# A fused two-block transformer kernel: state-space tables and sums moved to GpSimd, and the first norm's squares added by pairs

## What is computed

```python
def rms_norm(x, gain):
    y = x * rsqrt(mean(x * x, axis=-1) + EPS)
    return y * gain

def s5_mixer(h, w_in, lam_re, lam_im, log_step, b_re, b_im, c_re, c_im, d_skip, w_glu):
    u = (h @ w_in).reshape(bsz, seq, 64, 16)            # 64 groups of 16 channels
    step = exp(log_step)[:, None]
    a = exp(lr * step) * (cos(li * step) + i sin(li * step))   # 64 states in a group
    f = (a - 1) / (lr + i li)
    b = f * (b_re + i b_im)
    x_t = a * x_(t-1) + b @ u_t                           # along the sequence
    y = real(c @ x_t) + d_skip * u
    z = gelu(y)
    val, gate = split(z @ w_glu)
    return val * sigmoid(gate)

x = x + s5_mixer(rms_norm(x, mix_norm[0]), ...)
```

## Time and profile before

| | |
|---|---|
| median of 3 runs | 1765.92 us (1765.71 to 1766.07) |
| the profiled execution, its own time | 1765.68 us |
| its span | 1763.9 us |
| PE busy | 1734.0 us (98%) |
| DVE busy | 1244.0 us (71%) |
| ACT busy | 924.6 us (52%) |
| POOL busy | 486.6 us (28%) |
| granted TensorE clock | 0.998 of 2.4 GHz |

### The profile page before, as it was taken

How to read it: one execution, slowest core, us unless ns; L and a number is a source line. 1 busy time by engine, 2 the same in 40 slices (tenths; PEclk the granted TensorE clock), 3 DMA queues, 4 the chain that set the end, 5 groups by cost and what they waited for, 6 DMA issues and landing times.

```text
span 1763.9 us, 27676 instructions
## 1 busy us (share of the span) xinstructions
PE 1734.0 (98%) x10382; PEld 1420.9 (81%) x10382; DVE 1244.0 (71%) x1895; ACT 924.6 (52%) x1692; POOL 486.6 (28%) x383
## 2 busy tenths in 40 slices
PE   9999999999999999999999999999999999999997
PEld 6778899999887787789999988688667768866775
DVE  8964488887345888768888835565777586577757
ACT  6634466565224677556566522333667543366753
POOL 0870166775001000026776500132001113200110
PEclk9999999999999999999999999999999999999999
DMA  6332323223333211022323333233111123311111
GB/s 214 94 97 84 95 72 117 100 98 119 105 94 106 75 43 37 13 96 85 108 97 119 105 98 99 82 106 98 60 48 56 57 79 107 98 60 49 59 55 55
DMA packets 56465, 151.75 MB, mean 86 GB/s; under 512 B 16768, under 2 KB 18720, under 8 KB 56336
## 3 DMA queue, kind: packets, MB, share of 16 engines
q1 hardware_dynamic: 52816, 147.45, 25.7%
q0 software_dynamic: 3520, 2.57, 0.6%
HBM read 142.84 MB, written 4.19 MB: 83 GB/s over the span
## 4 chain that ended last, share of the span: by engine, by line
PE 87%; DVE 6%; POOL 3%; ACT 2%; issue 1%; DMA 0%; SPq 0%; DVEq 0%; POOLq 0%; ACTq 0%
PE bank L2587 10%; PE bank L2588 10%; PE bank L2589 10%; PE bank L2800 8%; PE bank L2801 8%; PE bank L2802 8%; PE bank L3218 3%; PE bank L3220 3%; PE bank L3219 3%; PE bank L2883 2%; PE bank L3171 2%; PE bank L3200 2%; PE bank L3202 2%; PE bank L3201 2%; PE bank L2915 1%
## 5 line engine op out<-in xcount | busy, mean ns | idle before, releaser
L1619 DVE TENSOR_TENSOR wl<-raw,wh 128x1024 fp32r<-128x1024 f32 (+2 forms) x183 | 230.2, 1258 | 240.9 <-ACT wh L864 236.7
L864 ACT ACTIVATE wh<-raw 128x1024 fp32r<-128x1024 f32 (+2 forms) x183 | 188.6, 1031 | 354.7 <-PE bank L2589 287.3
L2587 PE MATMUL bank<-hidH,wh 128*128 128x512 f32 x352 | 137.4, 390 | 0.0
L2588 PE MATMUL bank<-hidL,wh 128*128 128x512 f32 x352 | 137.0, 389 | 0.0
L2589 PE MATMUL bank<-hidH,wl 128*128 128x512 f32 x352 | 136.9, 389 | 0.0
L2800 PE MATMUL bank<-xH,wh 128*128 128x256 f32 x480 | 135.8, 283 | 0.0
L2801 PE MATMUL bank<-xL,wh 128*128 128x256 f32 x480 | 135.8, 283 | 0.0
L2802 PE MATMUL bank<-xH,wl 128*128 128x256 f32 x480 | 135.8, 283 | 0.0
L775 POOL TENSOR_TENSOR raw<-raw,wsum 128x512 f32<-128x512 f32 x40 | 86.5, 2163 | 115.6 <-DVE wl L1948 115.6
L3218 PE MATMUL bank<-xH,wh 128*128 128x512 f32 x256 | 111.3, 435 | 0.0
L3220 PE MATMUL bank<-xH,wl 128*128 128x512 f32 x256 | 100.8, 394 | 0.0
(11 more groups left out here) (525 smaller groups left out, 5112.9 us busy)
## 6 DMA issues: line engine op xcount, KB each, us to landing
raw<-w_gu_dram SPq DMA_DIRECT2D x88, 512.0 KB, 3.6
raw<-w_p_dram SPq DMA_DIRECT2D x64, 512.0 KB, 3.3
raw<-w_dn_dram SPq DMA_DIRECT2D x32, 448.0 KB, 3.4
raw<-w_glu_dram SPq DMA_DIRECT2D x16, 512.0 KB, 3.5
raw<-w_dn_dram SPq DMA_DIRECT2D x16, 512.0 KB, 3.6
raw<-w_out_dram SPq DMA_DIRECT2D x16, 512.0 KB, 3.2
raw<-w_in_dram SPq DMA_DIRECT2D x8, 512.0 KB, 7.7
raw<-w_o_dram SPq DMA_DIRECT2D x8, 512.0 KB, 3.2
```

The lines of the kernel that those rows point to most:

```text
L864: nc.scalar.activation(wh[:, (st.base + u) % 2, 0:kts * P], raw[:, (st.base + u) % 4, 0:kts * P], ACT.Copy).then_inc(w_high, 1)
L1619: nc.vector.tensor_tensor(wl[:, s, 0:kts * P], raw[:, (st.base + u) % 4, 0:kts * P], wh[:, s, 0:kts * P].bitcast(F32), ALU.subtract).then_ ...
L2587: nc.tensor.matmul(bank, wh[:, s, w], hi[:, k, :], start=first and kt == 0, stop=False)
L2588: nc.tensor.matmul(bank, wh[:, s, w], lo[:, k, :], start=False, stop=False)
```

## The change

Five things are done together.

- POOL adds the squares by pairs in place, and PE sums four tiles with the matrix of ones, not eight.
- The turn angles (32 activations on ACT, rounding and wrapping on DVE) become three operations of 2048 elements on POOL (`make_turns`).
- `input_sums` and `output_sums` go from DVE to POOL. The negated copy of Cz goes: ACT scales by -1 when it copies.
- g(1) goes from DVE to POOL, ahead of v(0). So that the count of `g_ready` keeps its order, POOL waits within v(0) until g(0) is there and then counts g(1).
- DVE makes the low part of block 3 before `gained`, and signals `powers_ready` right behind it. ACT takes the sines earlier, beside blocks 4 and 5.

```diff
@@ gpsimd @@
-            def make_v(q):
+            def make_v(q, between=None):
...
+                if between:
+                    between()
...
+            def make_turns():
+                each = vecs[:, VEC["chunk"]:VEC["chunk"] + NCH].unsqueeze(1).to_broadcast([P, NPAIR, NCH])
+                turn = v("turn").unsqueeze(2).to_broadcast([P, NPAIR, NCH])
+                pool.wait_ge(sem("vecs_loaded"), 16)
+                pool.wait_ge(sem("lrs_ready"), 2)
+                step(nc.gpsimd.tensor_tensor(Ei[:, :, :], each, turn, ALU.mult))
+                pool.sem_inc(sem("phases_ready"), 1)
+                step(nc.gpsimd.tensor_scalar(Er[:, :, :], Ei[:, :, :], ROUND, ROUND, ALU.add, ALU.subtract))
+                nc.gpsimd.tensor_tensor(Ei[:, :, :], Ei[:, :, :], Er[:, :, :], ALU.subtract).then_inc(sem("phases_ready"), 1)
+
+            def input_sums():
+                pool.wait_ge(sem("bc_loaded"), 32)
+                step(nc.gpsimd.tensor_tensor(Bz[:, 2, :, :], Bz[:, 0, :, :], Bz[:, 1, :, :], ALU.add))
+                step(nc.gpsimd.tensor_tensor(Bz[:, 3, :, :], Bz[:, 1, :, :], Bz[:, 0, :, :], ALU.subtract))
+                pool.sem_inc(sem("pool_tables"), 1)
+
+            def output_sums():
+                step(nc.gpsimd.tensor_tensor(Cz[:, 3, :, :], Cz[:, 0, :, :], Cz[:, 1, :, :], ALU.add))
+                step(nc.gpsimd.tensor_tensor(Cz[:, 4, :, :], Cz[:, 0, :, :], Cz[:, 1, :, :], ALU.subtract))
...
+            for j in range(4):
+                pool.wait_ge(sq_ready, 2 * j + 2)
+                step(nc.gpsimd.tensor_tensor(x_square(2 * j), x_square(2 * j), x_square(2 * j + 1), ALU.add))
+                pool.sem_inc(sem("pool_tables"), 1)
+            make_turns()
+            input_sums()
+            output_sums()
             pool.wait_ge(sem("powers_ready"), 1)
+            make_g(1)
+
+            def second_inputs():
+                pool.wait_ge(sem("g_ready"), 1)
+                pool.sem_inc(sem("g_ready"), 1)
+
             pool.wait_ge(sem("sq_used"), KD)
             pool.wait_ge(sd_ready, 1)
             pool.wait_ge(sem("phases_ready"), 3)
-            make_v(0)
+            make_v(0, between=second_inputs)
@@ scalar @@
-                    for ri, c in enumerate((0, 2)):
-                        ins = nc.scalar.activation(C2[halves(h), q % 2, ri, :, h, :], Cz[halves(h), c, q * QP:(q + 1) * QP, :], ACT.Copy)
+                    for ri, sign in enumerate((1.0, -1.0)):
+                        ins = nc.scalar.activation(C2[halves(h), q % 2, ri, :, h, :], Cz[halves(h), ri, q * QP:(q + 1) * QP, :], ACT.Copy, scale=sign)
...
-            for pair in range(NPAIR):
-                ins = nc.scalar.activation(Ei[:, pair, :], each, ACT.Identity, scale=v_turn(pair))
...
+            act.wait_ge(sem("pool_tables"), 1)
+            act.wait_ge(sem("bc_loaded"), 32)
+            lag_weights(0)
+            nc.scalar.preload_act_table(ACT.Sin)
             next_block(2)
-            act.wait_ge(sem("pool_tables"), 1)
-            lag_weights(0)
+            act.wait_ge(sem("phases_ready"), 3)
+            step(nc.scalar.activation(Er[:, :, :], Ei[:, :, :], ACT.Abs))
+            nc.scalar.activation(Er[:, :, :], Er[:, :, :], ACT.Sin, scale=-TURN, bias=tiny[:, 3:4]).then_inc(sem("phases_ready"), 1)
             next_block(3)
+            nc.scalar.activation(Ei[:, :, :], Ei[:, :, :], ACT.Sin, scale=TURN).then_inc(sem("phases_ready"), 1)
+            nc.scalar.preload_act_table(ACT.Gelu_apprx_tanh)
+            lag_weights(1)
             next_block(4)
@@ vector @@
             powers(4)
+            next_block(1)
             gained()
-            next_block(1)
-            input_sums()
-            output_sums()
+            dve.sem_inc(sem("powers_ready"), 1)
             dve.wait_ge(sd_ready, 1)
             take_input(0)
             take_input(1)
             next_block(2)
+            dve.wait_ge(sem("bc_loaded"), 32)
             make_g(0, (0,))
             take_input(2)
             next_block(3)
             make_g(0, (1,))
-            wrap_turns()
             take_input(3)
             next_block(4)
             take_input(4)
-            make_g(1, (0,), between=lambda: take_input(5))
-            make_g(1, (1,))
+            take_input(5)
@@ tensor @@
-                    for k in range(KD):
-                        pe.wait_ge(sq_ready, k + 1)
-                        nc.tensor.matmul(banks[7][:, :], const("ones"), x_square(k), start=k == 0, stop=k == KD - 1)\
-                          .then_inc(sem("sq_used"), 1)
+                    for j in range(4):
+                        pe.wait_ge(sem("pool_tables"), j + 2)
+                        nc.tensor.matmul(banks[7][:, :], const("ones"), x_square(2 * j), start=j == 0, stop=j == 3)\
+                          .then_inc(sem("sq_used"), 2)
```

More of the change, by code:

```diff
@@ L694, in make_g @@
                 step(nc.gpsimd.tensor_tensor(t, ps, br, ALU.mult))
-                pool.wait_ge(sem("lag_made"), 2 * q - 3)
-                pool.wait_ge(sem("wt_ready"), 4 * q - 4)
+                if q >= 2:
+                    pool.wait_ge(sem("lag_made"), 2 * q - 3)
+                    pool.wait_ge(sem("wt_ready"), 4 * q - 4)
                 step(nc.gpsimd.tensor_tensor(to[:, 0], pi, b_sum, ALU.mult))
@@ L699, in make_g @@
                 step(nc.gpsimd.tensor_tensor(to[:, 1], pr, b_gap, ALU.mult))
-                nc.gpsimd.tensor_tensor(to[:, 1], to[:, 1], t, ALU.add).then_inc(sem("g_ready"), 1)
+                if q == 1:
+                    step(nc.gpsimd.tensor_tensor(to[:, 1], to[:, 1], t, ALU.add))
+                else:
+                    nc.gpsimd.tensor_tensor(to[:, 1], to[:, 1], t, ALU.add).then_inc(sem("g_ready"), 1)
+            def make_turns():
[15 more added lines that the diff above has]
+                step(nc.gpsimd.tensor_tensor(Cz[:, 4, :, :], Cz[:, 0, :, :], Cz[:, 1, :, :], ALU.subtract))
             def v(name):
@@ L967, in _ @@
             next_block(1)
-            act.wait_ge(sem("lrs_ready"), 2)
-            each = vecs[:, VEC["chunk"]:VEC["chunk"] + NCH]
-            for pair in range(NPAIR):
-                ins = nc.scalar.activation(Ei[:, pair, :], each, ACT.Identity, scale=v_turn(pair))
-            ins.then_inc(sem("phases_ready"), 1)
             nc.scalar.preload_act_table_set("natural_log_exp_and_others")
@@ L979, in _ @@
               .then_inc(sem("act_made"), 1)
+            act.wait_ge(sem("pool_tables"), 1)
+            act.wait_ge(sem("bc_loaded"), 32)
+            lag_weights(0)
+            nc.scalar.preload_act_table(ACT.Sin)
             next_block(2)
-            act.wait_ge(sem("pool_tables"), 1)
-            lag_weights(0)
+            act.wait_ge(sem("phases_ready"), 3)
+            step(nc.scalar.activation(Er[:, :, :], Ei[:, :, :], ACT.Abs))
+            nc.scalar.activation(Er[:, :, :], Er[:, :, :], ACT.Sin, scale=-TURN, bias=tiny[:, 3:4]).then_inc(sem("phases_ready"), 1)
             next_block(3)
+            nc.scalar.activation(Ei[:, :, :], Ei[:, :, :], ACT.Sin, scale=TURN).then_inc(sem("phases_ready"), 1)
+            nc.scalar.preload_act_table(ACT.Gelu_apprx_tanh)
+            lag_weights(1)
             next_block(4)
             copy_w(0, (0, 1))
-            lag_weights(1)
-            nc.scalar.preload_act_table(ACT.Sin)
-            act.wait_ge(sem("phases_ready"), 3)
-            step(nc.scalar.activation(Er[:, :, :], Ei[:, :, :], ACT.Abs))
             act.wait_ge(w_split, st.base + 6 + 5)
@@ L992, in _ @@
             copy_w(0, (2, 3))
-            nc.scalar.activation(Er[:, :, :], Er[:, :, :], ACT.Sin, scale=-TURN, bias=tiny[:, 3:4]).then_inc(sem("phases_ready"), 1)
             clear_lags(first_MS)
@@ L997, in _ @@
             next_block(5)
-            nc.scalar.activation(Ei[:, :, :], Ei[:, :, :], ACT.Sin, scale=TURN).then_inc(sem("phases_ready"), 1)
-            nc.scalar.preload_act_table(ACT.Gelu_apprx_tanh)
             def turned_high(q, ts=(0, 1)):
@@ L1694, in chunk_turn @@
                 nc.vector.tensor_scalar(o, o, CH / TWO_PI, None, ALU.mult).then_inc(sem("lrs_ready"), 1)
-            def wrap_turns():
-                dve.wait_ge(sem("phases_ready"), 2)
-                step(nc.vector.tensor_scalar(Er[:, :, :], Ei[:, :, :], ROUND, ROUND, ALU.add, ALU.subtract))
-                nc.vector.tensor_tensor(Ei[:, :, :], Ei[:, :, :], Er[:, :, :], ALU.subtract).then_inc(sem("phases_ready"), 1)
             def denominator():
@@ L1743, in gained, with make_g @@
                     tt(table[:, 2, :, :], table[:, 0, :, :], table[:, 1, :, :], ALU.add)
-            def input_sums():
-                dve.wait_ge(sem("bc_loaded"), 32)
-                tt(Bz[:, 2, :, :], Bz[:, 0, :, :], Bz[:, 1, :, :], ALU.add)
-                tt(Bz[:, 3, :, :], Bz[:, 1, :, :], Bz[:, 0, :, :], ALU.subtract)
-            def output_sums():
-                step(nc.vector.tensor_scalar(Cz[:, 2, :, :], Cz[:, 1, :, :], -1.0, None, ALU.mult))
```

(11 more changed lines are left out.)

## The result

| | before | after |
|---|---|---|
| median of five runs each | 1765.92 us | 1784.07 us (1783.16 to 1784.82) |
| ratio | | 1.0103, 95% interval 1.0091 to 1.0114 |
| span of the profiled execution | 1763.9 us | 1781.4 us |

The forecast was 1786.0 us with a range of 1772 to 1794. The page of the changed kernel: its first line, the busy time of each engine, and PE's granted clock in 40 slices.

The account below looks back on a forecast made before the run. PE, busy 98% of the 1763.9 us span, was taken as the bound. g(0)'s transposes 24.0 us late less 4.8 of waits made 19.2 on 1765.68, 1784.9; with 1 for the clock, 1786 us, range 1772 to 1794.

Parts of the forecast that it names:

- The mechanism: DVE operations reading two SBUF tiles wait for POOL's whole current operation, small ones included; PE stands still 24 to 43 us.
- Rivals A: DVE's small operations beside POOL are not held; PE saves 3.2 us of sums, v(2) comes 3.5 us earlier: 1762.4; 12%.
- B: DVE's chain keeps its turn and POOL out; block 2 4 us late, POOL's list 10 us later: 8 us, 1774; 12%.
- Its ending: From g(0) on the lateness stays with PE, less waits; transposes at 70 instead of 45.95, 24.0 us later.
- The pair sums: Before block 2: POOL ends the fourth at about 20.3, PE asks at 20.7; the 3.2 us saved are worth nothing.
- The rounding: In POOL's early list: one input, 2048 elements, taken as 3.0 us between bounds of 1.9 and 4.4.
- DVE gets one for each of POOL's: Beside POOL's eleven operations: 15 of DVE's 33 small ones done at 37.8 us, low part of block 2 ends at 43.3.
- the low part of block 4: On DVE before g(0): held once by POOL's g(1), started at 50, ending near 57.5.
- What comes back: Behind g(0): PE's waits whose cause is now early go, 4.8 us off the lateness.
- The four waits of the earlier trace: PE's waits for g(3), v(2), take_input and g(1), up to 130 us: 1.5 + 1.4 + 1.2 + 0.7 = 4.8 us.
- The clock: PE slower after three standstills; a restart costs nothing to 2.3 us, 1 us taken since the last standstill is short.

Follow-up runs that it names:

- pool_reads: Kernel before plus eight multiplications of 128x1024 on POOL in a scratch tile behind the chunk turn, nothing of the change: 1778.36 us, ratio 1.0070.
- pool_clears: Kernel before plus nineteen POOL memsets of a scratch tile, which write SBUF and read nothing: 1766.28 us, ratio 1.0002.
- after_no_pairs: Changed kernel with the pair sums taken out again, so PE sums eight squares: 1780.01 us, ratio 1.0081.
- am_two_inputs: Changed kernel with one small DVE operation (am = ar - 1) written with two SBUF inputs and the same value: 1781.44 us, ratio 1.0089.
- round_in_halves: Changed kernel with POOL's rounding of 2048 elements written as two of 1024: 1779.91 us, ratio 1.0078.

## Why the prediction was right, step by step

**The mechanism** is shown: the small operations are held by POOL's. It is seen in 11 rows of the changed kernel, without the change's own work in `pool_reads`, and, but for one operation, not where POOL only writes (`pool_clears`). Rivals A (small ones not held) and B (a chain of DVE keeps POOL out) are wrong: POOL never waited for the chain. Its ending was right too: the lateness of DVE's list goes on to PE.

**The pair sums** were in time and PE's 3.2 us worth nothing, as said; alone they cost 4.2 us.

**The rounding was the term that was mis-sized**: 3.0 us taken, 1.9 to 4.4 as bounds, 7.10 measured. Memset and copy were the nearest rows, but have no arithmetic; with two steps POOL takes 3.5 ns for each of the 2048 elements. POOL's list therefore ended at 41.8, not 37.8. The other operations were well priced (turn product 3.66 against 4.1, subtraction 4.54 against 4.7, sums 1.25 to 1.32).

**"DVE gets one for each of POOL's"** was wrong the other way: 21 small operations were done at the end of POOL's list, not 15. Both errors together give 44.8 + 1.2 = 46.0 for the low part of block 2 (43.3 predicted), 52.5 for the powers (49.9), and 70.6 for g(0) (69.7). In between, the low part of block 4 was predicted to be held by 2.2 us and was held by 0.2 (56.53, 1.41 us), which took back most of the lateness; its end, 57.9, is near the 57.5 predicted.

**What comes back** was too small: 4.8 predicted, and 24.7 - 17.5 = 7.2 measured (the transposes' delay less the span's growth). The four waits of the earlier trace rows went, and with them others that the prediction had not counted, of 0.7 us at lag_turned, 0.5 at a second take_input and 0.4 in two more: 6.4 in all. The last 0.8 us lie at the same places: matmul by matmul, PE's lateness falls only there, from 24.7 to 17.6 us at 111 us of the kernel before, and in most places by up to 0.2 us more than the wait (0.80 at the wait of 0.67 for g(1)).

**The clock** fell, and cost nothing in this execution. The windows of the changed kernel (stretch, length, busy time of each engine, granted clock, DMA):

```profile
24.00:28.00 4.00, 0.32 (x1) 0.00 (x0) 3.93 (x3) 1.32 (x2) 3.78 (x2) 1.00 0.00 0
28.00:46.00 18.00, 0.00 (x0) 0.00 (x0) 17.28 (x23) 0.00 (x0) 13.39 (x6) 0.51 0.00 0
46.00:52.00 6.00, 5.83 (x14) 4.62 (x15) 5.59 (x15) 0.00 (x0) 0.00 (x0) 0.50 0.57 173
52.00:56.00 4.00, 4.00 (x19) 3.26 (x18) 1.82 (x4) 3.38 (x7) 3.25 (x2) 0.97 0.37 136
```

PE stood still from 24.3, the clock was 1.00 up to 28 and 0.51 from there to 46, the level of 1.2 GHz; and block 2 ran at 0.50 for 6 us before it was 1.00 again. But PE waited 2.14 us for DVE at 67.75 and 0.65 at 70.69, so these slower 6 us are covered. Behind the standstill of 2.14 us the clock stayed at 1.00, so the 1 us for it was not due here. That is partly luck, as `after_no_pairs` shows at the same place (two rows of PE):

```profile
63.38 0.47 PE L2595 MATMUL bank<-xH,wh 128*128 128x512 f32 x1 [2.40 <-DVE wl L1650]
...
66.47 1.71 PE L2636 MATMUL bank<-cons,G 128*128 128x128 f32 x8
```

There PE had stood still for 2.40 us, the granted clock was 0.61 from 64 to 66 and 0.54 to 68, and the transposes of g(0) took 1.71 us instead of 1.09, which no wait covers. The same is seen in `am_two_inputs` (1.70) and `round_in_halves` (1.57, and there PE began them at 66.65, though g(0) had been ready at 65.5). As an estimate from these rows, the first two would have gained some 0.7 us more without it, and the last 1.5. The other four executions of the changed kernel took 0.7 to 1.7 us more than the profiled one, at a mean granted clock of 0.990 instead of 0.991; whether the clock fell a second time in them no trace shows.

The sum as measured: 24.7 - 7.2 = 17.5 us on the span, against 24.0 - 4.8 + 1 = 20.2. The nearness of the number is in part luck: 2.7 us too little at block 2 and 2.2 of it taken back at block 4, then 2.4 us too little coming back and 1 us for the clock too much.

## What to carry to other kernels

An engine that is idle is not free: work that reads SBUF on GpSimd (POOL) costs VectorE (DVE), for each operation, up to that operation's whole length, and a chain of small dependent operations can pay once for each operation of GpSimd, as it did eleven times here. Place such work where VectorE works from PSUM or waits, and try long one-input operations in pieces: two of 1024 elements instead of one of 2048 gained 4.2 us here. Price an operation of GpSimd by a row with the same number of arithmetic steps, not by a copy.

## What the runs showed of the hardware that was not expected

- A one-input arithmetic operation on GpSimd with two steps takes 3.65 us for 1024 elements and 7.10 for 2048; with one step 2.78 for 1024; a copy of 1024 takes 1.07.
- It does not hold VectorE for its length. Of 1024 elements (2.78 or 3.65 us) it held the waiting operation until 1.1 to 1.2 us from its start, in six cases, about as long as the copy of 1024, which held to its end; of 2048 (7.1 us) a two-input operation for 4.5 us, in three cases, and a one-input operation to the end, in three (the third of each is in `after_no_pairs`). Why 2048 is not twice 1024 stays open. Operations of GpSimd with two inputs held to their end in all of these traces. The Trainium skill ("SBUF — State Buffer", "Who interferes with whom") says that whichever starts first has the port pair for the whole instruction; for GpSimd's two-input operations the rows agree; for its one-input arithmetic they do so only where a one-input operation of VectorE stood beside 2048 elements.
- At a handover GpSimd does not always win. VectorE's next small operation often passes in GpSimd's gap of 0.07 to 0.2 us between two operations (39.06 and 39.28 above: one passes, the next is held), which made two for each of GpSimd's where one had been assumed.
